# Third attention of a two-block transformer: two heads at a time, two pairs of score banks in turn, weight splits moved behind it

## The chip, the cores and the metric

One core of one Trainium2 chip. The metric is the device time of one execution in microseconds; the kernel before takes 1890.29 us (median of three runs, 1889.44 to 1892.73).

## The reference, cut to what matters

The program computes a whole two-block network on 256 tokens of width 1024. The change touches one part of it, the third of its attentions: 16 query heads of 64 share 2 key/value heads, each query sees the 128 latest keys, and a learned "sink" logit joins the softmax.

```python
def swa_mixer(x, w_qkv, sinks, w_out, pos):
    q, k, v = jnp.split(x @ w_qkv, SWA_SPLITS, axis=-1)
    q = partial_rope(q.reshape(B, S, N_HEADS_SWA, HEAD_DIM), pos)
    k = partial_rope(k.reshape(B, S, N_KV_SWA, HEAD_DIM), pos)
    ...
    o = sliding_window_gqa_sinks(q, k, v, sinks)
    return o.reshape(B, S, N_HEADS_SWA * HEAD_DIM) @ w_out

def sliding_window_gqa_sinks(q, k, v, sinks):
    s = jnp.einsum('bnqhgd,bnkhd->bnhgqk', qb, kk) * scale
    s = jnp.where(mask[None, :, None, None], s, -jnp.inf)
    mx = jnp.maximum(jnp.max(s, axis=-1), sink)
    e = jnp.exp(s - mx[..., None])
    w = e / (jnp.sum(e, axis=-1) + jnp.exp(sink - mx))[..., None]
    return jnp.einsum('bnhgqk,bnkhd->bqnhd', w, vv)
```

After it come the output projection (`c_out`), a layer norm, a mixture of 8 experts (more than half of the time) and a gated projection.

## The kernel before, in words

Each engine runs one program written out by hand, and semaphores tie them together. Products of 32-bit matrices are made in three passes: every weight chunk (128 x 2048) is loaded by SP's queue into one of four buffers `w_raw`, ScalarE rounds it to `w_hi` (`round_to`, L608), VectorE writes the rest to `w_lo` (the split, L1134), and TensorE multiplies `xt_hi` by `w_hi`, `xt_hi` by `w_lo` and `xt_lo` by `w_hi` (`rows_chunk`, L1920 to L1922). SP may load a chunk only once the chunk four places before it is split. `round_to(c)` on an engine means "do all chunks below c here". The chunks of the third attention are `c_sw` to `c_sw + 5` (block `kv`, then two query blocks `q0` and `q1`, two chunks each); `c_sw + 6` to `c_sw + 9` are those of `c_out`.

PSUM has 8 banks. Banks 0 to 3 are `acc`, two each for the even and the odd weight block; banks 4 to 7 are `scr`. The sixteen heads go in two groups g of eight. Of one head:

- TensorE, `swa_qk`: one mask matmul and two score matmuls per head, always for two heads, into banks of `scr`; then `at_qk` is raised. In a pair of these there are 2 mask matmuls and 4 score matmuls (the trace counts 8, two passes each).
- VectorE, `swa_max`: two maxima (L1429 over 128 keys, L1430 over 256 keys), a drain, and the negative maximum with the sink (L1432); then `at_negm`.
- ScalarE, `swa_prob`: two exponentials with their sums, a drain, then `at_p`. With `at_p` the score bank is free.
- TensorE, `swa_turn`: three transposes into bank `acc[q1][h % 2]`, after `at_p` of this head and the copy of the head two before; then `at_t`.
- VectorE, `turned_prob`: copies the 128 x 384 to SBUF (L1444); then `at_pt`.
- TensorE, `swa_pv`: three products with the values (L2401 to L2403), 64 wide, into `acc[q0]` for group 0 and banks 6 and 7 for group 1.

At a group's end VectorE's `attended` divides by the sums and writes `y` (L1456), TensorE transposes `y` (`turn_half`, `late_half`), ScalarE rounds the transposed half to `xt_hi` and VectorE writes `xt_lo` (`turned_at`). `rotate` is the rotary embedding of a query block on VectorE; ScalarE's `swa_block` copies a block out of PSUM before it, and `turned_queries` copies the transposed queries to `qk2` after it. `keep_warm(n)` issues n matmuls of 128x512 whose result nobody reads.

Of the kernel before, what the change touches and what calls it, by code (L numbers as in the profile page):

```python
# [23 lines left out]
P = 128  # L24
# [91 lines left out]
def build(nc, a, out, upto="end"):  # L116
# [27 lines left out]
    with ExitStack() as ctx:  # L144
# [125 lines left out]
        def swa_bank(g, h):  # L270

            return scr[:, (0, 1, 2, 3, 0, 1, 0, 1)[h] if g else h % 3, :]
# [329 lines left out]
        def _(act):  # L602
# [221 lines left out]
            def swa_prob(g, h):  # L824

                act.wait_ge(S("at_negm"), 8 * g + h + 1)
                b_, smx_ = swa_bank(g, h), smx2[:, g]
                for t, (c0, c1) in enumerate(((0, P), (P, SCW))):
                    copy((s_first, s_more)[g][:, h, c0:c1], b_[:, c0:c1], ACT.Exp, bias=smx_[:, 1, t, h:h + 1],
                         accum_out=smx_[:, 2, t, h:h + 1])  # L830
                act.drain().then_inc(S("at_p"), 1)
# [158 lines left out]
            if "qkv" in live:  # L990
# [40 lines left out]
                for t in range(NT):  # L1031
                    turned_at(8, t, 2 * t, acc[q0_b[0] % 2][t])
# [92 lines left out]
        def _(dve):  # L1125
# [299 lines left out]
            def swa_max(g, h):  # L1425

                b_, smx_ = swa_bank(g, h), smx2[:, g]
                dve.wait_ge(S("at_qk"), 8 * g + h + 1)
                dve.reduce_max(smx_[:, 0, 0, h:h + 1], b_[:, 0:P], AX_X)  # L1429
                dve.reduce_max(smx_[:, 0, 1, h:h + 1], b_[:, P:SCW], AX_X)  # L1430
                dve.drain()
                TS(smx_[:, 1, :, h:h + 1], smx_[:, 0, :, h:h + 1], sink[:, 8 * g + h:8 * g + h + 1], -1.0, ALU.max, ALU.mult)  # L1432
                dve.drain().then_inc(S("at_negm"), 1)

            def swa_sink(g):

                s8 = sink[:, 8 * g:8 * g + 8].unsqueeze(1).broadcast_to([P, NT, 8])
                TT(smx2[:, g, 3], s8, smx2[:, g, 1], ALU.add)
                dve.drain().then_inc(S("sink_ready"), 1)

            def turned_prob(g, h):

                dve.wait_ge(S("at_t"), 8 * g + h + 1)
                dve.tensor_copy(pt2[:, h % 2, :], acc[q1_b[0] % 2][h % 2][:, 0:SCW]).then_inc(S("at_pt"), 1)  # L1444
# [182 lines left out]
            if "qkv" in live:  # L1627
# [28 lines left out]
                dve.sem_inc(S("rotated"), 1)  # L1656
# [1001 lines left out]
```

## Time and profile before

| what | us |
|---|---|
| median of three runs | 1890.29 |
| the profiled execution, its own time | 1890.27 |
| its span, first to last instruction | 1888.5 |
| of it, up to the third attention's scores | 0 to 738.5 |
| scores, softmax and values of the third attention | 738.5 to 792.3 |
| output projection, norm, routing | 792.3 to 860 |
| experts and last projection | 860 to 1888.5 |

The profiled execution stands at the median of the runs. Lines in it are those of the kernel above; most ScalarE work has the helper line L608, so that its rows are told apart by their tiles (`s_first` and `s_more` are the probabilities of the two groups, `p` is `p2`, `pt` is `pt2`, `qk` is `qk2`).

### The profile page before, as it was taken

The page shows a single profiled execution, that of the slowest core. Times are in us where ns is not written, and L with a number is a line of the kernel's source. Part 1 is how long each engine was busy: PE and PEld are TensorE (multiplying, and loading weights), DVE is VectorE, ACT ScalarE, POOL GpSimd, SP SyncE. Part 2 cuts the span into 40 slices and gives each one's busy share as a digit, 9 for nine tenths or more (in the row PEclk, how much of TensorE's full clock was granted, in tenths as well). Part 3 has the DMA queues.
Part 4 walks back from the last instruction along what each step waited for, and adds up shares of the span by engine and source line. Part 5 has one row for each costly group of instructions (what it writes and reads, how often), then busy time and mean ns, then how long its engine had stood idle before and what let it go on. Part 6 is the DMA issues. An engine that isn't in the chain of part 4 may idle for free.

```text
span 1888.5 us, 24161 instructions
## 1 busy us (share of the span) xinstructions
PE 1834.6 (97%) x9844; PEld 1532.7 (81%) x9853; DVE 1394.3 (74%) x1231; ACT 1106.0 (59%) x989; POOL 61.4 (3%) x83
## 2 busy tenths in 40 slices
PE   8999999999999998899999999999999999999997
PEld 6979997897899876768788888888888888888875
DVE  4766775466645565578988888888888888888876
ACT  4545544374334344357667667676677766776772
POOL 2200000200000001000000000000000000000000
PEclk8999999999999999799999999999999999999998
DMA  7444546432555563049999999999999999999980
GB/s 250 157 153 155 178 167 212 152 129 90 174 188 180 190 206 115 24 163 387 350 367 356 344 371 349 363 363 350 369 359 341 367 352 361 364 336 375 366 307 24
DMA packets 248857, 491.02 MB, mean 260 GB/s; under 512 B 10422, under 2 KB 15610, under 8 KB 248752
## 3 DMA queue, kind: packets, MB, share of 16 engines
q1 hardware_dynamic: 244992, 477.30, 71.3%
q0 software_dynamic: 3328, 10.73, 1.7%
q8 instruction: 69, 1.13, 0.3%
q10 hardware_dynamic: 432, 1.57, 0.2%
q14 instruction: 36, 0.29, 0.0%
HBM read 487.46 MB, written 2.10 MB: 259 GB/s over the span
## 4 chain that ended last, share of the span: by engine, by line
PE 86%; DVE 8%; ACT 2%; DVEq 1%; issue 1%; DMA 0%; ACTq 0%; SPq 0%
PE psum L2518 16%; PE psum L2520 16%; PE psum L2519 16%; PE psum L1974 5%; PE psum L1977 5%; PE psum L1976 5%; PE psum L1920 5%; PE psum L1922 5%; PE psum L1921 5%; PE psum L1994 3%; DVE w_lo L1134 2%; DVE w_lo L1699 1%; ACT w_hi L608 1%; DVE xt_lo L1146 1%; DVE uv L1394 1%
## 5 line engine op out<-in xcount | busy, mean ns | idle before, releaser
L608 ACT ACTIVATE w_hi<-w_raw 128x2048 fp32r<-128x2048 f32 (+1 forms) x357 | 641.6, 1834 | 107.1 <-PE psum L1922 60.2
L1699 DVE TENSOR_TENSOR w_lo<-w_raw,w_hi 128x2048 fp32r<-128x2048 f32 (+1 forms) x238 | 511.5, 2189 | 75.3 <-ACT w_hi L608 75.2
L1134 DVE TENSOR_TENSOR w_lo<-w_raw,w_hi 128x2048 fp32r<-128x2048 f32 (+2 forms) x119 | 261.4, 2228 | 138.5 <-ACT w_hi L608 137.0
L2518 PE MATMUL psum<-w_hi,xg_hi 128*128 128x512 f32 x892 | 357.6, 401 | 1.0 <-DVE w_lo L1699 1.0
L2520 PE MATMUL psum<-w_hi,xg_lo 128*128 128x512 f32 x892 | 353.5, 396 | 0.0
L2519 PE MATMUL psum<-w_lo,xg_hi 128*128 128x512 f32 x892 | 353.5, 396 | 0.0
L1699 DVE TENSOR_TENSOR w_lo<-raw_more,w_hi 128x2048 fp32r<-128x2048 f32 (+1 forms) x118 | 254.6, 2197 | 34.8 <-ACT w_hi L608 34.5
L1974 PE MATMUL psum<-xt_hi,w_hi 128*128 128x256 f32 (+1 forms) x976 | 276.2, 283 | 1.4 <-DVE w_lo L1134 0.6
L1977 PE MATMUL psum<-xt_hi,w_lo 128*128 128x256 f32 (+1 forms) x976 | 275.7, 282 | 0.0
L1976 PE MATMUL psum<-xt_lo,w_hi 128*128 128x256 f32 (+1 forms) x976 | 274.8, 282 | 0.0
L608 ACT ACTIVATE w_hi<-raw_more 128x2048 fp32r<-128x2048 f32 (+1 forms) x118 | 212.7, 1839 | 19.3 <-PE psum L2520 18.5
L2520 PEld LDWEIGHTS psum<-w_hi,xg_lo 128*128 128x128 f32 x892 | 167.9, 188 | 40.7
L2518 PEld LDWEIGHTS psum<-w_hi,xg_hi 128*128 128x128 f32 x892 | 168.1, 188 | 40.5 <-DVE w_lo L1699 1.9
L2519 PEld LDWEIGHTS psum<-w_lo,xg_hi 128*128 128x128 f32 x892 | 168.2, 189 | 38.5
L1974 PEld LDWEIGHTS psum<-xt_hi,w_hi 128*128 128x128 f32 (+1 forms) x976 | 182.7, 187 | 4.6 <-issue 1.9
L1976 PEld LDWEIGHTS psum<-xt_lo,w_hi 128*128 128x128 f32 (+1 forms) x976 | 182.7, 187 | 0.5
L1977 PEld LDWEIGHTS psum<-xt_hi,w_lo 128*128 128x128 f32 (+1 forms) x976 | 181.6, 186 | 0.3
L2518 PE MATMUL psum<-w_hi,mh_hi 128*128 128x512 f32 x448 | 179.1, 400 | 0.2 <-DVE w_lo L1699 0.2
L2520 PE MATMUL psum<-w_hi,mh_lo 128*128 128x512 f32 x448 | 177.6, 397 | 0.0
L2519 PE MATMUL psum<-w_lo,mh_hi 128*128 128x512 f32 x448 | 177.4, 396 | 0.0
L608 ACT ACTIVATE mg<-psum 128x512 f32<-128x512 f32 x56 | 33.6, 599 | 175.4 <-PE psum L2520 175.4
L1920 PE MATMUL psum<-w_hi,xt_hi 128*128 128x512 f32 (+1 forms) x256 | 103.3, 404 | 5.0 <-DVE xt_lo L1146 3.6
(394 smaller groups left out, 2144.1 us busy)
## 6 DMA issues: line engine op xcount, KB each, us to landing
w_raw<-in_moe_w_gate_up SPq DMA_DIRECT2D x150, 1024.0 KB, 7.5
raw_more<-in_moe_w_gate_up SPq DMA_DIRECT2D x74, 1024.0 KB, 7.6
w_raw<-in_moe_w_down SPq DMA_DIRECT2D x64, 1024.0 KB, 7.4
raw_more<-in_moe_w_down SPq DMA_DIRECT2D x32, 1024.0 KB, 7.1
w_raw<-in_w_up SPq DMA_DIRECT2D x22, 1024.0 KB, 5.5
w_raw<-in_ffn_w_gate_up SPq DMA_DIRECT2D x22, 1024.0 KB, 5.5
w_raw<-in_w_in SPq DMA_DIRECT2D x12, 1024.0 KB, 5.7
w_raw<-in_ab_w_in SPq DMA_DIRECT2D x12, 1024.0 KB, 5.3
```

Source lines behind the costliest of these rows:

```text
L608: return act.activation(o, i, func, **kw)
L1134: TT(w_lo[:, k % RING, 0:n], raw(slot, n), w_hi[:, k % RING, 0:n].bitcast(F32), ALU.subtract)\
L1699: TT(w_lo[:, at, 0:n], raw(slot, n), w_hi[:, at, 0:n].bitcast(F32), ALU.subtract).then_inc(S("lo_ready"), 1)
L1920: mm(o, hi(k, t), wh, start=(k == ps[0][0]), stop=False)
L1921: mm(o, hi(k, t), wl, start=False, stop=False)
L1922: m = mm(o, lo(k, t), wh, start=False, stop=(k == kmax))
L1974: mm(o, w_hi[:, slot, cols], xt_hi[:, k, :], start=(k == 0 and c_ % 2 == 0), stop=False, skip_group_check=True)
L1976: mm(o, w_hi[:, slot, cols], xt_lo[:, k, :], start=False, stop=False, skip_group_check=True)
L1977: m = mm(o, w_lo[:, slot, cols], xt_hi[:, k, :], start=False, stop=(k == KD - 1), skip_group_check=True)
L2518: mm(o, hi[:, q, :], wh, start=(q == first), stop=False)
L2519: mm(o, hi[:, q, :], wl, start=False, stop=False)
L2520: m = mm(o, lo[:, q, :], wh, start=False, stop=(q == last))
```

## The change: heads by pairs

All three engines now step by pairs p = 0 to 7 (two heads each).

- The scores of pair p go to banks 4 and 5, then 6 and 7, in turn; pair 7 goes to banks 2 and 3 (`acc[q0]`), after `at_y`, that is once the first group's result has been taken from there. Pair 1's scores have a bank pair of their own, so they wait for no probability; pair p's scores wait for `at_p` of pair p - 2.
- `swa_max` takes both heads in one instruction per key range (128x2x128 and 128x2x256), and one instruction with a negated sink makes the two negative maxima.
- `swa_prob` does both heads' four exponentials before its one drain and signal.
- `swa_turn` makes six transposes into banks 0 and 1 (`acc[q1]`) and waits for the copy of the pair before; `turned_prob` copies both heads (128x768) at once; `swa_pv` makes six products. The transposes thus have one pair of banks instead of two single banks in turn.
- ScalarE copies block q1 right after pair 0's probabilities (before: after five heads), VectorE rotates it after two pairs' maxima and before any copy (before: after eight heads' maxima and one copy), TensorE turns its queries right behind pair 0's transposes. 4 warming matmuls stand there instead of 8.
- VectorE splits chunk `c_sw + 6` after all maxima and seven of the eight copies (before: after three heads' maxima), and `c_sw + 7` after the last copy; ScalarE rounds `c_sw + 7` after the probabilities instead of between the groups.
- The first transposed half of `y` goes to banks 4 and 5 instead of `acc[q0]`.

The core of the diff, cut:

```diff
+        def swa_pair(p):
+            b_ = (4, 6, 4, 6, 4, 6, 4, 2)[p]
+            return psum[:, b_:b_ + 2, 0:SCW]
...
 (ScalarE)
-                for h in range(5):
-                    swa_prob(0, h)
+                swa_prob(0)
                 swa_block(q1_b)
-                for h in range(5, 8):
-                    swa_prob(0, h)
-                turned_queries(4, 7)
+                swa_prob(1)
+                turned_queries(4, 6)
                 turned_queries(6, 7)
+                for p in range(2, 4):
+                    swa_prob(p)
                 swa_sink(0)
-                round_to(c_sw + 8)
-                for h in range(8):
-                    swa_prob(1, h)
+                for p in range(4, 8):
+                    swa_prob(p)
                 swa_sink(1)
...
                 round_to(c_sw + 9)
 (VectorE)
+            def swa_max(p):
+                g, hs = p // 4, slice(2 * (p % 4), 2 * (p % 4) + 2)
+                dve.wait_ge(S("at_qk"), 2 * p + 2)
+                dve.reduce_max(smx2[:, g, 0, 0, hs], swa_pair(p)[:, :, 0:P], AX_X)
+                dve.reduce_max(smx2[:, g, 0, 1, hs], swa_pair(p)[:, :, P:SCW], AX_X)
+                dve.drain()
+                STT(smx2[:, g, 1, :, hs], smx2[:, g, 0, :, hs], -1.0, sink[...], ALU.mult, ALU.min)
+                dve.drain().then_inc(S("at_negm"), 1)
+            def turned_prob(p):
+                dve.wait_ge(S("at_t"), p + 1)
+                dve.tensor_copy(pt2[:], turned_pair[:, :, 0:SCW]).then_inc(S("at_pt"), 1)
...
+                swa_max(0)
+                swa_max(1)
                 wait_evacuated(dve, q1_b[0])
                 rotate(NB, 8)
+                for p in range(4):
+                    turned_prob(p)
+                    swa_max(p + 2)
+                    if p == 1:
+                        swa_sink(0)
+                turned_prob(4)
                 attended(0)
+                swa_max(6)
+                turned_prob(5)
+                swa_max(7)
+                turned_prob(6)
                 swa_sink(1)
+                round_to(c_sw + 7)
+                for t in range(NT):
+                    turned_at(8, t, 2 * t, scr[:, t, :])
+                turned_prob(7)
                 round_to(c_sw + 8)
                 attended(1)
 (TensorE)
+                    if 5 <= k < 7:
+                        swa_qk(k - 5)
                 rows_chunk(q1_b, 1, xh, xl, between=scores_between)
+                swa_qk(2)
                 wait_evacuated(pe, q1_b[0])
+                swa_turn(0)
+                keep_warm(4, 3)
+                pe.wait_ge(S("at_p"), 2)
+                turn_queries(4, 6)
                 turn_queries(6, 7)
+                swa_pv(0)
+                swa_turn(1)
+                for p in range(1, 6):
+                    swa_qk(p + 2)
+                    swa_pv(p)
+                    swa_turn(p + 1)
+                for t in range(NT):
+                    turn_half(y, 0, t, scr[:, t, :])
+                swa_pv(6)
+                swa_turn(7)
+                swa_pv(7)
```

TensorE, one round of the steady part. Before, two heads of the second group, with the semaphores on which each row waits; a row without a name for one follows the row before it:

```order
L2378 MATMUL psum<-mask_126,ident_127 128x384 [waits at_p]
L2378 MATMUL psum<-mask_126,ident_127 128x384
L2381 MATMUL psum<-qk_123 128x128 x2
L2381 MATMUL psum<-qk_123 128x256 x2
L1994 MATMUL psum<-ident,s_first 128x128 [waits at_pt,at_p]
L1994 MATMUL psum<-ident,s_first 128x128 x2
L2401 MATMUL psum<-p_122,pt_124 128x64 [waits at_pt]
L2402 MATMUL psum<-p_122,pt_124 128x64
L2403 MATMUL psum<-p_122,pt_124 128x64
L1994 MATMUL psum<-ident,s_first 128x128 [waits at_pt,at_p]
L1994 MATMUL psum<-ident,s_first 128x128 x2
L2401 MATMUL psum<-p_122,pt_124 128x64 [waits at_pt]
```

and in the changed kernel, one pair:

```order
L2384 MATMUL psum<-mask_126,ident_127 128x384 [waits at_p]
L2384 MATMUL psum<-mask_126,ident_127 128x384
L2387 MATMUL psum<-qk_123 128x128 x2
L2387 MATMUL psum<-qk_123 128x256 x2
L2413 MATMUL psum<-p_122,pt_124 128x64 [waits at_pt]
L2414 MATMUL psum<-p_122,pt_124 128x64
L2415 MATMUL psum<-p_122,pt_124 128x64
L2413 MATMUL psum<-p_122,pt_124 128x64
L2414 MATMUL psum<-p_122,pt_124 128x64
L2415 MATMUL psum<-p_122,pt_124 128x64
L1996 MATMUL psum<-ident,s_first 128x128 [waits at_pt,at_p]
L1996 MATMUL psum<-ident,s_first 128x128 x5
```

The same matmuls for two heads now stand in three runs, scores, products, transposes, with one wait each. Between a transpose and the product that needs its copy stand the scores of a later pair, where before there was one head's transposes at most places.

VectorE at the end of the stage. Before, from the last copy but four:

```order
L1438 TENSOR_TENSOR smx_131<-sink,smx_131 128x16
L1134 TENSOR_TENSOR w_lo<-w_raw,w_hi 128x2048 [waits hi_ready]
L1444 COPY pt_124<-psum 128x384 [waits at_t] x3
L1153 TENSOR_TENSOR xt_lo<-psum,xt_hi 128x4x128 [waits xt_hi_ready] x2
L1444 COPY pt_124<-psum 128x384 [waits at_t]
L1450 TENSOR_TENSOR smx_131<-smx_131 128x16 [waits at_sum]
```

and in the changed kernel, from the last copy but one:

```order
L1449 COPY pt_124<-psum 128x768 [waits at_t]
L1443 TENSOR_TENSOR smx_131<-smx_131,sink 128x16
L1138 TENSOR_TENSOR w_lo<-w_raw,w_hi 128x2048 [waits hi_ready]
L1157 TENSOR_TENSOR xt_lo<-psum,xt_hi 128x4x128 [waits xt_hi_ready] x2
L1449 COPY pt_124<-psum 128x768 [waits at_t]
L1138 TENSOR_TENSOR w_lo<-w_raw,w_hi 128x2048 [waits hi_ready]
L1455 TENSOR_TENSOR smx_131<-smx_131 128x16 [waits at_sum]
```

One split (`c_sw + 6`) and both parts of `xt_lo` now stand between the last two copies, and a second split (`c_sw + 7`) between the last copy and the second `attended`.

## Rows read from the trace of the kernel before

**Rows 1.** The page: busy us of each engine (share) xinstructions.

```profile
PE 1834.6 (97%) x9844; PEld 1532.7 (81%) x9853; DVE 1394.3 (74%) x1231; ACT 1106.0 (59%) x989; POOL 61.4 (3%) x83
```

**Rows 2.** TensorE's waits from 738.5 to 792.5: total us, times, longest.

```profile
PE psum L2401 <- DVE pt L1444: 6.5, 7, 2.2
PE psum L2378 <- ACTq L831: 3.8, 3, 2.9
```

**Rows 3.** Windows: busy us (instructions) by engine, granted clock, DMA share, GB/s.

```profile
746.70:749.64 2.94, 0.00 (x1) 0.01 (x1) 2.46 (x9) 1.83 (x8) 0.00 (x0) 1.00 0.52 163
749.64:753.30 3.66, 3.63 (x16) 2.18 (x16) 1.27 (x5) 2.37 (x9) 0.00 (x0) 0.54 0.41 158
...
770.50:773.90 3.40, 1.29 (x10) 0.98 (x9) 2.92 (x9) 0.92 (x4) 0.00 (x0) 0.99 0.00 0
773.90:794.30 20.40, 18.12 (x80) 16.06 (x81) 11.40 (x24) 5.95 (x16) 0.00 (x0) 0.50 0.16 52
```

**Rows 4.** TensorE in time: start, us, line, operation; at the full clock.

```profile
738.52 0.50 PE L2378 MATMUL psum<-mask,ident 128*128 128x384 bf16 x2
...
739.81 0.50 PE L1920 MATMUL psum<-w_hi,xt_hi 128*128 128x512 f32 x1
...
741.97 0.50 PE L2378 MATMUL psum<-mask,ident 128*128 128x384 bf16 x2 [0.49 <-ACTq L831]
...
755.47 1.67 PE L1999 MATMUL psum<-ones_tri 128*128 128x512 bf16 x7
756.98 0.60 PE L1994 MATMUL psum<-ident,p 128*128 128x128 f32 x4
757.42 0.49 PE L1994 MATMUL psum<-ident,s_first 128*128 128x128 f32 x3
757.75 0.33 PE L2401 MATMUL psum<-p,pt 128*128 128x64 f32 x2
...
758.36 0.61 PE L1994 MATMUL psum<-ident,p 128*128 128x128 f32 x4
...
759.75 0.49 PE L2378 MATMUL psum<-mask,ident 128*128 128x384 bf16 x2
...
761.02 0.55 PE L1994 MATMUL psum<-ident,s_first 128*128 128x128 f32 x3
```

**Rows 5.** TensorE in time, the stage's end; at the half clock.

```profile
791.08 0.63 PE L2401 MATMUL psum<-p,pt 128*128 128x64 f32 x2
...
792.32 0.77 PE L1920 MATMUL psum<-w_hi,xt_hi 128*128 128x512 f32 x1
```

**Rows 6.** VectorE in time: maxima, a split, the first `attended`.

```profile
739.98 0.29 DVE L1429 TENSOR_REDUCE smx<-psum 128x1 f32<-128x128 f32 x1 [5.29 <-PE psum L2381]
740.19 0.41 DVE L1430 TENSOR_REDUCE smx<-psum 128x1 f32<-128x256 f32 x1
...
741.03 0.29 DVE L1429 TENSOR_REDUCE smx<-psum 128x1 f32<-128x128 f32 x1
...
744.40 2.29 DVE L1134 TENSOR_TENSOR w_lo<-w_raw,w_hi 128x2048 fp32r<-128x2048 f32 x1
...
771.69 0.17 DVE L1450 TENSOR_TENSOR smx<-smx 128x16 f32<-128x16 f32 x1
...
773.67 0.29 DVE L1429 TENSOR_REDUCE smx<-psum 128x1 f32<-128x128 f32 x1
```

**Rows 7.** VectorE groups of 380 to 560 us: shapes, busy, mean ns.

```profile
L1550 DVE COPY pt<-psum 128x384 f32<-128x384 f32 x8 | 4.4, 554 | 4.3 <-PE psum L1994 4.3
...
L1476 DVE TENSOR_TENSOR stick<-psum,mask_sb 128x768 f32<-128x768 f32 x4 | 3.8, 956 | 0.4 <-PE psum L2213 0.2
```

**Rows 8.** ScalarE in time, one head's exponentials and the next.

```profile
740.98 0.37 ACT L608 ACTIVATE s_first<-psum,smx 128x128 f32<-128x128 f32 x1 [1.32 <-DVEq L1433]
...
742.02 0.37 ACT L608 ACTIVATE s_first<-psum,smx 128x128 f32<-128x128 f32 x1
```

**Rows 9.** TensorE's waits after 860 us.

```profile
PE psum L2518 <- DVE w_lo L1699: 0.2, 1, 0.2
```

More of the change, by code:

```diff
@@ L2370, in turn_queries, with swa_qk @@
                     i.then_inc(S("swa_t"), 1)
-                def swa_qk(g, h):
-                    if g or h >= 2:
-                        pe.wait_ge(S("at_p"), (8, 8, 10, 14)[h // 2] if g else h - 1)
-                    pair = (h, h + 1)
-                    for u in pair:
-                        mm(swa_bank(g, u)[:, 0:SCW], ident_16[:], mask_16[:], start=True, stop=True)
+                def swa_qk(p):
+                    if p >= 2:
+                        pe.wait_ge(S("at_p"), p - 1)
+                    if p == 3:
+                        pe.wait_ge(S("qk2_ready"), 5)
+                    if p == SWA_PAIRS - 1:
+                        pe.wait_ge(S("at_y"), 1)
+                    g, to = p // 4, swa_pair(p)
+                    for u in range(2):
+                        mm(to[:, u, :], ident_16[:], mask_16[:], start=True, stop=True)
@@ L2379, in swa_qk @@
                     for t, (c0, c1) in enumerate(((0, P), (P, SCW))):
-                        for u in pair:
-                            i = mm(swa_bank(g, u)[:, c0:c1], qk2[lane(u), 4 * g + u // 2, t * P:(t + 1) * P],
-                                   qk2[lane(u), 8 + g, 0:c1 - c0], start=False, stop=True, skip_group_check=True)
+                        for u in range(2):
+                            i = mm(to[:, u, c0:c1], qk2[lane(u), p, t * P:(t + 1) * P], qk2[lane(u), 8 + g, 0:c1 - c0],
+                                   start=False, stop=True, skip_group_check=True)
@@ L2399, in swa_pv @@
+                def swa_pv(p):
+                    pe.wait_ge(S("at_pt"), p + 1)
+                    g = p // 4
+                    if p == 4:
+                        pe.wait_ge(S("at_p"), 6)
                     v = lambda t: p2[:, t, SWA_V + g * DH:SWA_V + (g + 1) * DH]
                     to = [scr[:, 2 + t, :] for t in range(NT)] if g else acc[q0_b[0] % 2]
-                    mm(to[0][:, o], pt2[:, h % 2, 0:P], v(0), start=True, stop=True)
-                    mm(to[1][:, o], pt2[:, h % 2, P:SEQ], v(0), start=True, stop=False)
@@ L2403, in swa_pv @@
-                    m = mm(to[1][:, o], pt2[:, h % 2, SEQ:SCW], v(1), start=False, stop=True)
-                    if h == 7:
+                    for u in range(2):
+                        o = slice((2 * (p % 4) + u) * DH, (2 * (p % 4) + u + 1) * DH)
+                        mm(to[0][:, o], pt2[:, u, 0:P], v(0), start=True, stop=True)
+                        mm(to[1][:, o], pt2[:, u, P:SEQ], v(0), start=True, stop=False)
+                        m = mm(to[1][:, o], pt2[:, u, SEQ:SCW], v(1), start=False, stop=True)
@@ L2405, in swa_pv @@
+                    if p % 4 == 3:
                         m.then_inc(S("at_o"), 1)
```

109 lines of the change are left out of this document (23 added, 86 removed).

## The prediction

> **What bounds the kernel now.** The page first: TensorE is busy 97% of the span [rows 1], so the end moves only by what TensorE's program gains or loses, and only where it stands still or runs slowly. The list of waits for the stage of the third attention's scores, softmax and values shows where it stands still: ten stops with 10.3 us in total, seven for VectorE's copy of the transposed probabilities (6.5 us) and three for ScalarE's probabilities, whose banks the next scores need (3.8 us) [rows 2]. The windows show where it runs slowly: after the stop of 746.70 to 749.64 the granted clock is half until about 753.3, and after the window 770.5 to 773.9, in which TensorE was busy 1.29 of 3.40 us, it is half, 1.2 GHz, up to 794.3 [rows 3]. The reader is to see in rows 3 that in this last stretch TensorE is busy 18.12 of 20.40 us and the clock still does not rise; it does only when the dense weight products of `c_out` have run for 2 us, from 792.32 [rows 3, 5]. So a stop costs twice here, once itself and once by the slow clock behind it.
>
> The stage reaches from TensorE's first scores, 738.52 [rows 4], to the first product of `c_out`, 792.32 [rows 5]: 53.8 us. In pieces, at the full clock, by differences of starts in rows 4: the scores of two heads 1.27 (759.75 to 761.02), three transposes 0.33 (757.42 to 757.75), a head's products 0.61 (757.75 to 758.36), four transposes of queries or of `y` 0.44 (756.98 to 757.42), a warming matmul 0.22 to 0.24 (seven in 1.67), six weight products between scores 1.5 (739.81 to the stop that ends at 741.97 after 0.49). The work is then 8 x 1.27 + 16 x 0.33 + 16 x 0.61 + 4 x 0.44 + 8 x 0.22 + 2 x 1.5 = 31.8. The half clock adds 1.7 in 749.64 to 753.3 (3.63 busy for one pair's scores and six transposes, 1.93) and half of what is busy from 773.9 to 792.32, 18.12 less the 2.0 behind 792.32, so 8.1: together 9.8 [rows 3, 5]. With 10.3 of stops that is 51.9; the missing 1.9 I put down to the tail and the restart at ten stops, 0.2 each.
>
> **The change, part by part.** *Work on TensorE:* the same matmuls, four warming ones fewer: -0.9.
>
> *A steady round.* TensorE needs 1.27 + 2 x 0.61 + 2 x 0.33 = 3.15 for a pair. VectorE: a head's maxima come every 1.05 us (739.98 to 741.03) [rows 6]; from 128 to 256 elements a maximum grows from 0.29 to 0.41, so a pair's two grow by 0.12 and 0.27, together 1.45. A copy of 128x384 takes 0.554, and the nearest row to one of 128x768 is an addition from PSUM of that size, 0.956 [rows 7]. Bounds for the paired copy: not under 0.9 (the slope of rows 6 over 384 more elements, 0.36, on 0.554), not over 1.11 (two copies); I take 0.96, since element count sets both rows. VectorE's round is 2.4 us. ScalarE needs 1.04 for a head (740.98 to 742.02) [rows 8], so a pair at most 2.08, and with one drain fewer some 1.85. Both are below 3.15: TensorE sets the round, if no chain does. Chain one: six transposes end, 0.1 to VectorE, copy 0.96, 0.05 back, 1.1 to 1.2, against the 1.27 of scores that stand between: it fits by 0.1. With the copy at 1.11 it just misses and costs up to 0.1 a round. Chain two: scores, 0.1, maxima to ScalarE 1.00 + 0.39 (739.98 to 740.98, plus the growth) [rows 6, 8], probabilities 1.8, so 3.3, against 4.4 us of other work before that pair's transposes: it fits by 1.1.
>
> The Trainium skill (Perfetto Trace Analysis, Optimizing Scalar/DVE Operations) counts about 125 ns of overhead for each VectorE instruction on PSUM and says that larger ones help if the engine is saturated. By it 8 copies and 16 maxima fewer give an estimate of 3 us, and nothing if VectorE isn't the bound; VectorE is busy 1.27 of 3.66 us in the first slow stretch [rows 3], so the rule would price the edit near nothing. Rows 6 and 7 put the saving at about 0.15 per merged instruction, but what counts is whom a pair releases, and when.
>
> *The stops, followed in time.* Pair 1's scores wait for nothing now (0.5 gone), pair 2's wait for `at_p` of pair 0, ready at 743.2, before TensorE comes at 744.2. ScalarE copies block q1 when it ends (744.4), 1.0 us, VectorE rotates it for 1.85 (as now), so the queries can be turned at 747.4; TensorE has six transposes and four warming matmuls until 747.0 and waits 0.4. That replaces the stop of 2.94 [rows 3] and the 1.3 behind it. The split of `c_sw + 6`, 2.29 [rows 6], that stood between heads 2 and 3 of VectorE's maxima, at 744.40, is out of that chain. Then rounds of 3.15 without a stop until pair 5. There the first `attended`, 1.98 on VectorE (771.69 to 773.67) [rows 6], stands before pair 6's maxima and pair 5's copy: TensorE waits 0.9 for the copy, then 0.3 for the next one. By this count, restarts aside, its transposes of pair 7 are issued at 770.2.
>
> *The last stop is new.* Behind pair 6's copy VectorE splits `c_sw + 6` (2.29), makes two `xt_lo` (0.6 each at their pace) and only then copies pair 7, so 2.3 + 1.2 + 1.0 = 4.5 from 768.4: 772.9. TensorE waits 2.7. Behind it are only pair 7's products and `c_out`, whose operands are ready by then. The split of `c_sw + 7` ends at 775 and `attended` delivers at 776.4, before `c_out` has got to the transposes that want it, 2.8 us of products after 774.1 at the full clock: hidden, by 0.5. SP's load of the first expert chunk waits for the split of `c_sw + 6` and so starts 24 us later (770.7 for 746.7); it is needed only behind `c_out`, whose own weight products take over 22 us, and the routing, so hidden too.
>
> All stops: 0.4 + 0.9 + 0.3 + 2.7 + 0.3 of small ones = 4.6, with seven restarts of 0.1.
>
> *The clock.* With no early stop over 1 us I expect it full up to the last stop. That one, 2.7, is like the 2.94 after which it fell. Then pair 7's products take 2.4 instead of 1.2 (791.08 to 792.32 is one head's, 1.24) [rows 5], and `c_out` begins slow, as it does now. So half clock: 9.8 before, 1.2 after.
>
> **The sum.** Stops 4.6 for 10.3, -5.7; restarts 0.7 for 1.9, -1.2; half clock 1.2 for 9.8, -8.6; warming -0.9: -16.4. Behind the stage nothing absorbs it: after 860 us TensorE waits once, 0.2 us, for a weight split [rows 9]. The profiled execution took 1890.27, as the median: 1890.3 - 16.4 = 1873.9.
>
> **The rivals.** *The clock stays up to the end* (the last stop falls otherwise than the 2.94 did, as the 1.3 of 753.3 left it up): 1.2 less, and `c_out`'s first twelve products, about 1.0 slow now, at full pace: 1871.7. I give it 0.32, and the forecast 0.44.
>
> *VectorE or ScalarE is the bound of the round:* copies at 1.11 or more and maxima 0.2 dearer: five rounds and the last chain lose 0.3 to 0.5 each, so 1876.5. Against it: rows 7. 0.10.
>
> *The clock falls midway,* at the stop of 0.9 for pair 5's copy: 5.9 us of work behind it take twice as long, some 2.5 of which hides the last stop: +3.4, 1877.5; a fall one or two rounds earlier 3 us more each, 1880 to 1884. For it: transposes and narrow products did not raise the clock in 20 us [rows 3]. 0.09.
>
> *Slower:* the same mechanism from the start. The clock falls while TensorE waits for ScalarE's copy and the rotation (745.5 to 747.4) and stays half up to `c_out`: 24.1 us of work from 745.4 on double, 4.2 of stops are swallowed: +19.9 against a gain of 17.6 at full clock, 1892.6, and past 0.2% with a rotation 1.5 us later than counted. It decides once 17.6 us of work run slow. Against it: 0.4 of stop for the 2.94 that it took before. 0.03, of it 0.02 beyond 0.2%.
>
> *The gain does not reach the end,* since the late splits hold `c_out` or the experts' loads start late: then 3 to 17 us are lost, 1877 to 1890. Against it: the margins above. 0.02.
>
> **How the numbers follow.** The two likeliest cases span 1870.5 to 1875 with the copy's bounds; 8 in 10 need some of the third and the fourth: 1870 to 1879.5. Runs before spread by 3.3 us, and 0.2%, 3.8 us, is about what a measurement can tell from no change. Faster by more: 0.95; within: 0.03; slower: 0.02.
>
> **What would show it.** In the profile after: no stop over 1 us on TensorE before pair 7's products; rounds of 3.1 to 3.3 us; the pair's copy at 0.96, its maxima 0.41 and 0.68; a stop of 2 to 3.5 us before the last six products with VectorE in split, `xt_lo`, copy; the clock full up to there; `c_out`'s first product near 776. Wrong it would be with half clock inside the rounds, stops for `at_p`, or waits on w_lo in `c_out`.

## The result and the profile after

The changed kernel takes 1876.64 us, median of four runs (1872.35 to 1877.07); the kernel before, run beside it, 1889.87 (1887.90 to 1892.73). The ratio is 0.992 with a 95% interval of 0.9904 to 0.9936. In a second set it took 1875.78 against 1891.67, ratio 0.9924 (0.991 to 0.9937). It is faster, by 13 to 16 us; 1873.9 was forecast, with 1870.0 to 1879.5 as its range.

The kernel before has no single time either: beside the experiments its medians were 1888.12, 1891.48 and 1891.67. In the last of these sets six executions took 1886.76 to 1888.23, with a mean granted clock of 0.988 to 0.991, and eleven 1891.40 to 1893.36, with 0.985 to 0.987. Of the changed kernel's ten executions one took 1872.35, the others 1875.30 to 1877.07.

The profiled execution took 1876.83, its span is 1874.7. On its page TensorE is as full as in [rows 1], with 7.5 us less of busy time, and VectorE and ScalarE have lost little:

```profile
PE 1827.1 (97%) x9840; PEld 1527.8 (81%) x9849; DVE 1388.8 (74%) x1200; ACT 1105.0 (59%) x989; POOL 61.6 (3%) x83
```

TensorE's waits from 738 to 790 (total us, times, longest), the list that answers to [rows 2]:

```profile
PE psum L2413 <- DVE pt L1449: 3.3, 3, 2.3
PE psum L1996 <- DVEq L1648: 0.2, 1, 0.2
```

Ten stops with 10.3 us have become four with 3.45 (0.15, 0.78, 0.18 and 2.34), none of them for ScalarE's probabilities. The windows, in the columns of [rows 3], show the clock full (1.00) while the stops are short, and half behind the last one:

```profile
770.00:775.00 5.00, 2.48 (x21) 2.07 (x19) 4.88 (x7) 4.45 (x5) 0.00 (x0) 1.00 0.17 31
775.00:776.00 1.00, 1.00 (x7) 1.00 (x7) 1.00 (x1) 0.45 (x1) 0.00 (x0) 0.62 1.03 401
776.00:782.00 6.00, 6.00 (x18) 5.01 (x19) 2.78 (x5) 0.00 (x0) 0.92 (x1) 0.50 0.79 265
782.00:783.00 1.00, 1.00 (x8) 0.79 (x7) 0.00 (x0) 0.06 (x1) 0.00 (x0) 0.97 0.02 2
```

TensorE in time: rounds, the last stops, the stage's end, and the half transposes of `y` that follow `c_out`'s first twelve products.

```profile
751.68 0.49 PE L2384 MATMUL psum<-mask,ident 128*128 128x384 bf16 x2
752.10 0.93 PE L2387 MATMUL psum<-qk 64*128 64x128 f32 x8
752.95 0.43 PE L2413 MATMUL psum<-p,pt 128*128 128x64 f32 x2
...
754.34 0.82 PE L1996 MATMUL psum<-ident,s_first 128*128 128x128 f32 x6
755.00 0.49 PE L2384 MATMUL psum<-mask,ident 128*128 128x384 bf16 x2
...
767.10 0.43 PE L2413 MATMUL psum<-p,pt 128*128 128x64 f32 x2 [0.78 <-DVE pt L1449]
...
774.91 0.43 PE L2413 MATMUL psum<-p,pt 128*128 128x64 f32 x2 [2.34 <-DVE pt L1449]
...
777.23 0.77 PE L1922 MATMUL psum<-w_hi,xt_hi 128*128 128x512 f32 x1
...
782.31 0.60 PE L1996 MATMUL psum<-ident,y 128*128 128x128 f32 x4
```

The reader is to see three things. A round (one pair's scores, another's products, a third's transposes) is 3.32 us (751.68 to 755.00), without a stop; the first stop inside a round is the 0.78 at 767.10, behind the first `attended`. The stop before pair 7's products is 2.34, and those products then take 2.32 (774.91 to 777.23). And `c_out`'s twelve products need 5.08 up to 782.31. In the trace of before the same point is this row, 3.78 behind the first product of [rows 5]:

```profile
796.10 0.60 PE L1994 MATMUL psum<-ident,y 128*128 128x128 f32 x4
```

From this point on the time is the same: 1092.4 us remain to the end of the span in both traces (1888.5 - 796.10, 1874.7 - 782.31).

VectorE in time says why the last stop is there: the pair's copy stands behind a split and two `xt_lo`.

```profile
766.96 0.41 DVE L1433 TENSOR_REDUCE smx<-psum 128x2 f32<-128x256 f32 x1
767.29 0.68 DVE L1434 TENSOR_REDUCE smx<-psum 128x2 f32<-128x512 f32 x1
...
770.50 2.29 DVE L1138 TENSOR_TENSOR w_lo<-w_raw,w_hi 128x2048 fp32r<-128x2048 f32 x1
772.71 1.28 DVE L1157 TENSOR_TENSOR xt_lo<-psum,xt_hi 128x512 fp32r<-128x512 f32 x2
773.91 0.95 DVE L1449 COPY pt<-psum 128x768 f32<-128x768 f32 x1
774.78 2.28 DVE L1138 TENSOR_TENSOR w_lo<-w_raw,w_hi 128x2048 fp32r<-128x2048 f32 x1
```

The span is 13.8 us shorter, in three pieces: the stage from first scores to `c_out`'s first product takes 37.37 instead of 53.80 (739.86 to 777.23), -16.4; the twelve products take 5.08 instead of 3.78, +1.3; and the stage begins at 739.86 instead of 738.52, +1.3, though nothing ahead of it was changed.

### The profile page after: what moved, and what is told of

Read it like the earlier page. It is cut to its first block, busy times and chain, and to the rows that moved or that the text cites. A ratio compares the mean times of both kernels' runs of the same rounds, so it can differ in the third digit from the quotient of the medians.

```text
span 1874.7 us, 24092 instructions
## 1 busy us (share of the span) xinstructions
PE 1827.1 (97%) x9840; PEld 1527.8 (81%) x9849; DVE 1388.8 (74%) x1200; ACT 1105.0 (59%) x989; POOL 61.6 (3%) x83
## 4 chain that ended last, share of the span: by engine, by line
PE 87%; DVE 7%; ACT 2%; issue 1%; DVEq 1%; DMA 0%; ACTq 0%; SPq 0%
PE psum L2511 17%; PE psum L2513 17%; PE psum L2512 17%; PE psum L1976 5%; PE psum L1979 5%; PE psum L1978 5%; PE psum L1922 5%; PE psum L1923 5%; PE psum L1924 5%; PE psum L1996 3%; DVE w_lo L1138 2%; ACT w_hi L611 1%; DVE w_lo L1701 1%; DVE uv L1398 1%; PE psum L2485 1%
## 5 line engine op out<-in xcount | busy, mean ns | idle before, releaser
L611 ACT ACTIVATE w_hi<-raw_more 128x2048 fp32r<-128x2048 f32 (+1 forms) x118 | 212.7, 1838 | 19.0 <-PE psum L2513 18.5
```

The source lines that it names most:

```text
L611: return act.activation(o, i, func, **kw)
```

## The experiments

All times are medians. "Stage" is from the first scores to `c_out`'s first product, "twelve" the twelve products behind it, both in the run's one profiled execution. "Before" is the median of the kernel before in the same set; the ratio compares the runs of one set and is not the quotient of the two medians. The changed kernel itself stood in the first and in the last set only (a2_again), so differences of less than some 2 us between other rows and it are read from stage and twelve.

| run | us | before | ratio to before, 95% | stage | twelve |
|---|---|---|---|---|---|
| before (profile) | | | | 53.80 | 3.78 |
| changed | 1876.64 | 1889.87 | 0.992 [0.9904, 0.9936] | 37.37 | 5.08 |
| e1_fill | 1872.44 | 1888.12 | 0.9907 [0.9887, 0.9927] | 36.43 | 2.89 |
| e2_split_first | 1872.68 | 1888.12 | 0.991 [0.9891, 0.9929] | 35.13 | 2.89 |
| e3_both_splits | 1876.91 | 1888.12 | 0.9933 [0.9914, 0.9952] | 39.85 | 3.81 |
| e4_one_pair | 1885.88 | 1888.12 | 0.9977 [0.9965, 0.999] | 48.47 | 4.42 |
| b1_split_alone | 1888.5 | 1891.48 | 0.9992 [0.9981, 1.0004] | 50.64 | 2.89 |
| e5_single_ops | 1876.76 | 1891.48 | 0.9921 [0.99, 0.9942] | 37.88 | 5.05 |
| e6_block_late | 1875.47 | 1891.48 | 0.9921 [0.9903, 0.994] | 38.02 | 4.43 |
| e7_no_stop | 1874.24 | 1891.48 | 0.9908 [0.9891, 0.9925] | 35.17 | 4.51 |
| a2_again | 1875.78 | 1891.67 | 0.9924 [0.991, 0.9937] | 37.39 | 5.07 |
| e2_again | 1872.6 | 1891.67 | 0.9902 [0.9886, 0.9918] | 35.15 | 2.88 |
| b2_fill | 1887.66 | 1891.67 | 0.9983 [0.9974, 0.9992] | 49.16 | 4.39 |
| e8_own_buffer | 1871.43 | 1891.67 | 0.9896 [0.988, 0.9912] | 33.89 | 2.89 |

**e1_fill: ten warming matmuls in the last stop.**

```diff
                 swa_turn(7)
+                keep_warm(10, 3)
                 swa_pv(7)
```

> The changed kernel with ten warming matmuls (128x512, bank 3) issued behind pair 7's transposes, in the last stop of 2.34 us. Nothing waits for them. Theory (a stop costs itself and then the slow clock behind it): the time until pair 7's products stays as it is, but the granted clock stays full there and in c_out; pair 7's products take 1.3 instead of 2.3 us and the first twelve products of c_out 2.8 instead of 4.8, so 3.0 us less than the changed kernel in a run like its profile (1877 to 1874). Rival (the clock falls for the long run of transposes and narrow products, not for the stop): the half clock comes all the same, 0 us. Second rival (the fillers only push the products back): up to 0.2 us more.

The filler takes 2.32 us, a stop of 0.18 remains, pair 7's products take 1.36 and the clock is 1.00 from 770 to 790:

```profile
771.01 2.32 PE L2001 MATMUL psum<-ones_tri 128*128 128x512 bf16 x10
773.51 0.43 PE L2413 MATMUL psum<-p,pt 128*128 128x64 f32 x2 [0.18 <-DVE pt L1449]
...
774.87 0.48 PE L1922 MATMUL psum<-w_hi,xt_hi 128*128 128x512 f32 x1
```

The filler does no work and takes as long as the stop, and 0.94 are gained in the stage and 2.19 in the twelve products, 3.1 together. So the half clock was a consequence of the standstill, and cost 3.1 us in the changed kernel. All four executions stand between 1870.77 and 1873.06, where nine of the changed kernel's ten took 1875.30 or more.

**e2_split_first, and again as e2_again: the split of `c_sw + 6` ahead of pair 0's maxima.**

```diff
                 dve.drain()
+                round_to(c_sw + 7)
                 swa_max(0)
```

> The changed kernel with the split of chunk c_sw+6 ahead of pair 0's maxima, where VectorE idles 5.2 us, instead of behind pair 6's copy. Theory: pair 0's maxima are some 0.7 us later and nobody waits for it; the last stop loses the 2.3 us of the split down to the bare chain of transposes, copy, products, so 2.34 becomes 1.0 to 1.3, and at that length the clock stays full: 1.2 + 3.0 = 4 us less than the changed kernel, about 1872.5. Rival: the stop gets shorter but the clock falls all the same, only 1.2 us less. Rival: the early split delays pair 0's probabilities so that a stop appears at pair 2's scores or the rotation, and 0.5 to 1 us of it is given back.

> The changed kernel with the split of c_sw + 6 ahead of pair 0's maxima, again, to have it beside the changed kernel in one set: 4 us less than the changed kernel by my theory (1.3 of stop, 1.0 in pair 7's products, 1.9 in the first twelve products of c_out), the stop of 1.05 again with the clock up behind it. If the clock falls behind it this time, 1 to 2 us less.

The last stop is 1.05 in both profiles, the clock stays at 1.00 to 790, and VectorE's 2.29 us there delay nobody. In the last set, beside the changed kernel, 1872.60 against 1875.78: 3.2 less where 4 were expected. Stage and twelve are 2.2 shorter each, 4.4 in all, but this profile reached the stage 1.6 later than that of a2_again (740.32 against 738.70). The waits of the first:

```profile
PE psum L2414 <- DVE pt L1449: 2.0, 3, 1.0
PE psum L1997 <- DVEq L1648: 0.2, 1, 0.2
```

**e3_both_splits: the split of `c_sw + 7` ahead of pair 7's copy too,** so that the last stop doubles.

```diff
-                turned_prob(7)
                 round_to(c_sw + 8)
+                turned_prob(7)
```

> The changed kernel with the split of c_sw+7 ahead of pair 7's copy as well: the suspected delay of the last stop doubled. Theory: the last stop grows by 2.2 us to 4.6; behind it the clock is half as already now, so 2.2 us more than the changed kernel, up to 1 more if the half clock lasts longer. Rival (the stop is not on the path, as TensorE would wait for c_out's operands anyway): 0.

The wait and the window:

```profile
PE psum L2413 <- DVE pt L1449: 5.5, 3, 4.5
```

```profile
774.00:780.00 6.00, 4.11 (x16) 3.82 (x17) 3.30 (x6) 0.23 (x1) 0.00 (x0) 0.50 0.86 302
```

2.2 us more of stop make the stage 2.5 longer but the twelve products 1.3 shorter, since the clock fell near 773.7, inside the stop, and part of its slow time passed while TensorE stood. Together that is 1.2 more. The median is 0.3 above the changed kernel's in the first set and 1.1 above that in the last, in neither case the +2.2 that I expected: a longer stop doesn't price the slow clock behind it anew.

**e4_one_pair: the scores of pair p wait for the probabilities of pair p - 1,** as if there were one pair of score banks.

```diff
                     if p >= 2:
-                        pe.wait_ge(S("at_p"), p - 1)
+                        pe.wait_ge(S("at_p"), p)
```

> The changed kernel, but the scores of pair p wait for the probabilities of pair p-1 instead of pair p-2, as if there were one pair of score banks. Theory (two pairs in turn are what keeps TensorE from stopping): the chain scores, maxima, probabilities, 3.3 us, has then to fit into one pair's products and transposes, 1.9 us, so five rounds stop 1.3 to 1.6 us each, 7 to 8 us in all, and more with a slower clock, up to 15: 1884 to 1892, most of the gain gone. Rival (pairing of instructions is the gain, banks are not): under 2 us.

Six stops for ScalarE come back, the largest, 2.81, at the place of the 2.94 of [rows 3], and behind it the clock is at 0.55 in 748 to 755:

```profile
PE psum L2384 <- ACTq L836: 8.2, 6, 2.8
PE psum L2413 <- DVE pt L1449: 2.3, 1, 2.3
```

```profile
748.00:755.00 7.00, 7.00 (x32) 4.62 (x32) 2.14 (x5) 0.55 (x2) 0.00 (x0) 0.55 0.00 1
```

11.1 of the 16.4 us of the stage go, 7.1 of them as stops (10.5 for 3.45), as expected, and the rest by the clock, which is half again from 778.2 to 781.5. With everything else of the change in place, the second bank pair so carries two thirds of the gain, the half clock that it keeps away included. How much that clock weighs varies: two of the ten executions took 1879.88 and 1880.00, with a mean granted clock of 0.992 and 0.993, the other eight 1885.43 to 1887.17, with 0.989 or 0.990.

**b1_split_alone: the kernel before, with only the split of `c_sw + 6` moved ahead of the maxima.**

```diff
+                round_to(c_sw + 7)
-                for h in range(3):
-                    swa_max(0, h)
-                round_to(c_sw + 7)
-                for h in range(3, 8):
+                for h in range(8):
                     swa_max(0, h)
```

> The kernel before, with one thing of the change alone: VectorE's split of chunk c_sw + 6 stands ahead of the first head's maxima instead of between heads 2 and 3. My theory (the chain per head and three banks make the early stop, the split only lengthens it): head 3's maxima come 2.2 us earlier, but head 4's scores end at about 746.7 as now, so its maxima come at 746.7, its probabilities end near 748.6 and the scores of heads 6 and 7 start at 748.7 instead of 749.64; the stop of 2.94 becomes 2.0, and the time falls by 1 us, by at most 3 if the clock stays up behind the shorter stop, up to some 10 us if it stays up to the end. Rival (most of the change's gain is the split's place, not the pairs): the stop vanishes, the clock never falls early, and the time comes near that of the changed kernel, 12 to 14 us less.

TensorE, at the scores of heads 6 and 7:

```profile
749.38 0.52 PE L2376 MATMUL psum<-mask,ident 128*128 128x384 bf16 x2 [2.01 <-ACTq L831]
```

The stop is 2.01, as counted, and the interval of the ratio holds 1, so the rival, 12 to 14 us less, is wrong. The split made the stop longer, it did not make it. That the chain per head with its three banks did is what is left; for the banks e4_one_pair shows it, in the order by pairs. Another stop grew, since the early split delays the first maxima, and the stops of the stage sum to 10.8, for 10.3:

```profile
742.64 0.50 PE L2376 MATMUL psum<-mask,ident 128*128 128x384 bf16 x2 [1.17 <-ACTq L831]
```

Yet the stage of this profile is 3.2 shorter. Its last stretch of half clock, behind stops of the same lengths as before (1.31 and 2.23), ended at 783.8 and not at 794.3:

```profile
774.00:783.60 9.60, 7.73 (x34) 6.06 (x35) 5.08 (x12) 3.55 (x14) 0.00 (x0) 0.50 0.00 0
```

Whether the split or the single execution did that isn't shown. Five of the ten executions took 1886.28 to 1887.47 and five 1889.52 to 1891.22, two groups like those of the kernel before.

**e5_single_ops: order and signals by pairs, VectorE's instructions per head.**

```diff
-                dve.reduce_max(smx2[:, g, 0, 0, hs], swa_pair(p)[:, :, 0:P], AX_X)
-                dve.reduce_max(smx2[:, g, 0, 1, hs], swa_pair(p)[:, :, P:SCW], AX_X)
+                for u in range(2):
+                    h = 2 * (p % 4) + u
+                    dve.reduce_max(smx2[:, g, 0, 0, h:h + 1], swa_pair(p)[:, u, 0:P], AX_X)
+                    dve.reduce_max(smx2[:, g, 0, 1, h:h + 1], swa_pair(p)[:, u, P:SCW], AX_X)
...
-                dve.tensor_copy(pt2[:], turned_pair[:, :, 0:SCW]).then_inc(S("at_pt"), 1)
+                for u in range(2):
+                    i = dve.tensor_copy(pt2[:, u], turned_pair[:, u, 0:SCW])
+                i.then_inc(S("at_pt"), 1)
```

> The changed kernel with its order and its signals by pairs, but VectorE's instructions per head again: four maxima of a pair instead of two, two copies of 128x384 (0.55 each at their own pace) instead of one of 128x768. A pair's maxima then take about 1.36 instead of 1.10 and its copy 1.11 instead of 0.96. My theory (TensorE sets the round, the order is what gains): the copy still ends within 0.1 us of when TensorE has done the scores in between; 0 to 0.1 per round, 0.3 at the first attended and 0.15 to 0.4 at the last stop: 0.5 to 1 us slower than the changed kernel. Rival (fewer and larger VectorE instructions are what gains): 3 us slower or more, with VectorE's busy time in the stage up by that and stops of TensorE for the copy in each round.

The pair's two copies take 1.02 for 0.96, the stage is 0.5 longer, the waits for the copy are 3.6 for 3.3, at the same three places, and no round has got a new one. So of the 16.4 us the merging of VectorE's instructions brings 0.5; the rest is banks, order and the signals by pairs. (ScalarE's exponentials stayed by pairs in this run.)

```profile
770.45 1.02 DVE L1452 COPY pt<-psum 128x384 f32<-128x384 f32 x2 [1.01 <-PE psum L2000]
```

**e6_block_late: ScalarE's copy of block q1 behind pair 1's exponentials.**

```diff
-                swa_block(q1_b)
                 swa_prob(1)
+                swa_block(q1_b)
```

> The changed kernel with ScalarE's copy of block q1 behind pair 1's exponentials, not ahead of them. Pair 1's maxima are there at 745.35, so the copy starts near 747.1 instead of 745.64 and TensorE stops some 1.3 us before pair 0's transposes and 0.3 to 0.4 at the queries, 1.5 us in all. My theory (what matters is that a stop early in the stage stays short; the clock stayed up behind stops of 1.05 us): plus 1.5 us if the clock stays up; rival, in which a stop of 1.3 to 1.5 is already enough to lose the clock at the start: half clock from the first rounds on, 3 to 17 us more than the changed kernel.

```profile
PE psum L2413 <- DVE pt L1449: 3.3, 3, 2.3
PE psum L1996 <- ACT p L611: 1.6, 1, 1.6
PE psum L1996 <- DVEq L1648: 0.2, 1, 0.2
```

```profile
745.00:750.00 5.00, 3.27 (x26) 2.08 (x22) 2.63 (x12) 2.28 (x9) 0.00 (x0) 1.00 0.01 2
...
777.00:780.00 3.00, 3.00 (x9) 2.31 (x8) 2.21 (x5) 0.00 (x0) 0.09 (x1) 0.53 0.60 179
```

The new stop is there, 1.6, and the clock stays at 1.00 behind it; the rival that it would fall is wrong here. But the time didn't rise by 1.5 (the median is 1.2 below the changed kernel's in the first set, 0.3 below that in the last): behind the last stop, again 2.34, the clock fell only in 777 to 778 and pair 7's products still ran in 1.36, which gave 1.0 back, and the twelve gave 0.65. The same stop, in the same place of the program, was followed by 6.8 us of half clock in the two profiles of the changed kernel and by 3.4 in this one and in that of e4_one_pair.

**e7_no_stop: on top of the early split, the half transposes of `y` between pair 7's transposes and its products, and pair 7's copy ahead of the `xt_lo`.**

```diff
+                round_to(c_sw + 7)
                 swa_max(0)
...
+                turned_prob(7)
                 for t in range(NT):
                     turned_at(8, t, 2 * t, scr[:, t, :])
-                turned_prob(7)
...
-                for t in range(NT):
-                    turn_half(y, 0, t, scr[:, t, :])
                 swa_pv(6)
                 swa_turn(7)
+                for t in range(NT):
+                    turn_half(y, 0, t, scr[:, t, :])
                 swa_pv(7)
```

> The changed kernel with the split of c_sw + 6 ahead of pair 0's maxima, and at the end the products of pair 6 and the transposes of pair 7 ahead of the four half transposes of y on TensorE, and pair 7's copy ahead of the two xt_lo on VectorE. The early split alone left a stop of 1.05 us. Now the copy starts when pair 7's transposes end and lies beside 0.9 us of half transposes: the stop falls to 0.2 to 0.4, so 0.7 us less than with the early split alone, about 5 us less than the changed kernel. Rival: the xt_lo, now 1 us later, hold the first product of c_out back by as much, and nothing is gained over the early split alone.

TensorE's rows with a wait behind 770:

```profile
770.66 0.43 PE L2414 MATMUL psum<-p,pt 128*128 128x64 f32 x2 [1.05 <-DVE pt L1449]
773.92 0.43 PE L2414 MATMUL psum<-p,pt 128*128 128x64 f32 x2 [0.18 <-DVE pt L1449]
779.83 0.66 PE L1997 MATMUL psum<-ident,y 128*128 128x128 f32 x4 [1.43 <-DVEq L1465]
```

A miss that neither theory had. The stop of 1.05 is gone from pair 7 and has come at pair 6, whose copy the half transposes had covered before: there are 0.9 us of cover for two copies. And VectorE's split now began at 776.26, 36.1 us after the first scores, where it began 33.8 after them with the early split alone, so the second `attended` behind it was late for `c_out`: 1.43. The `xt_lo` held the first product back by nothing (it follows pair 7's products, 775.32), so the rival's cause is wrong too. The stage is no shorter than with the early split alone (35.17 for 35.13), and the twelve are 1.6 longer, most of it the new stop.

**a2_again: the changed kernel, unchanged.**

> The changed kernel once more, unchanged, beside the others of this set. In its first profile the stage began 1.3 us later than before, and its time ahead differs from that of before by the granted clock alone: 0.91 in 130 to 150 us, behind the same stop of about 4 us that left it at 1.00 in other profiles. My theory (whether a given stop drops the clock is not the same in each execution of one program): the times fall into groups 3 to 5 us apart, the stage starts near 738.4 or 740 according to the clock at 130 to 150, and the length of the half clock behind the last stop is again between 3 and 7 us. Rival: the same program has the same clock in each execution; then start and slow stretch are those of the first profile within 0.2 us.

The window 130 to 150, first of the changed kernel's first profile, then of this one, and TensorE at 140:

```profile
130.00:150.00 20.00, 16.59 (x98) 11.79 (x98) 13.46 (x19) 9.29 (x15) 1.07 (x2) 0.91 0.39 125
```

```profile
130.00:150.00 20.00, 15.96 (x106) 11.48 (x106) 12.84 (x18) 9.15 (x15) 1.07 (x2) 1.00 0.43 144
```

```profile
140.53 1.97 PE L1996 MATMUL psum<-ident,y 128*128 128x128 f32 x8 [2.65 <-DVEq L1196]
```

```profile
140.00 1.09 PE L1996 MATMUL psum<-ident,y 128*128 128x128 f32 x8 [2.65 <-DVEq L1196]
```

Behind the same stop of 2.65 the same eight transposes take 1.97 in one execution and 1.09 in the other, and the stage starts at 739.86 or 738.70. Of these 1.2 us half, 0.5, is there ahead of the transposes already (140.53 for 140.00), where the clock of the kernel's first microseconds rose at 20.9 in one execution and at 19.7 in the other. So the 1.3 us that the first profile had lost ahead of the stage are no effect of the change. Stage and twelve are as before (37.39, 5.07), and the last half clock lasts 6.8 again. The times did not fall into groups in this set (1875.30 to 1876.69); there my expectation missed, though the first set had one at 1872.35.

**b2_fill: the kernel before, with filler in three stops.**

```diff
+                def fill(n):
+                    for _ in range(n):
+                        mm(psum[:, 7, 256:512], busy[:, 0:P], busy[:, 256:512], start=True, stop=True)
+
+                fill(24)
                 swa_qk(0, 6)
...
+                fill(10)
                 swa_pv(1, 0)
                 swa_turn(1, 2)
+                fill(18)
                 swa_pv(1, 1)
```

> The kernel before with narrow filler products (128x256 into a free half bank, 0.11 us each) in three of its stops: 24 ahead of the scores of heads 6 and 7 (2.94 us), 10 ahead of head 8's products (1.31), 18 ahead of head 9's (2.23). The order by heads and all other instructions stay. My theory (about half the change's gain is clock, and a fast clock needs only that the stops be short or filled): the clock stays at full through the stage, the 9.8 us of half clock go, and 1 to 3 us come back as longer stops for the copies, which the slow TensorE had hidden behind 776: 1881 to 1884. Rival (the slow clock comes of the narrow work itself, not of the stops): the clock falls all the same, and the time is that of before or up to 1 us more.

```profile
742.00:785.00 43.00, 35.96 (x276) 26.64 (x277) 28.34 (x79) 21.92 (x74) 0.00 (x0) 1.00 0.08 27
785.00:792.00 7.00, 7.00 (x32) 6.42 (x31) 3.94 (x8) 0.00 (x0) 0.69 (x1) 0.54 0.43 144
```

```profile
PE psum L2401 <- DVE pt L1444: 5.7, 7, 1.9
PE psum L2378 <- ACTq L831: 1.1, 3, 0.5
```

The mechanism is right: full clock to 785, where the narrow work of before had half of it for 20 us. The size is wrong: 1881 to 1884 was expected, 1887.66 came. The stage is 4.6 shorter, not 9.8. The stops are now 6.8 and the fillers 6.2, 13.0 for 10.3, so 2.7 came back as waiting, as expected. But the clock fell after all behind late stops of 1.21 and 1.43, at 785.6, which costs 1.8 in the stage and 0.6 in the twelve products, and this profile began the stage 1.4 later than that of before. Of the 8.0 us that the clock gave back in the stage 2.7 returned as waiting and 0.7 aren't accounted for. So in the order by heads about a third of them was cover for VectorE's and ScalarE's chains: there a fast clock turns in part into waiting.

**e8_own_buffer: the early split, pair 7's copy in a buffer of its own, its transposes ahead of pair 6's products.**

```diff
-                dve.tensor_copy(pt2[:], turned_pair[:, :, 0:SCW]).then_inc(S("at_pt"), 1)
+                dve.tensor_copy(s_first[:, 0:2, :] if p == 7 else pt2[:], turned_pair[:, :, 0:SCW]).then_inc(S("at_pt"), 1)
...
+                turned_prob(7)
                 for t in range(NT):
                     turned_at(8, t, 2 * t, scr[:, t, :])
-                turned_prob(7)
-                round_to(c_sw + 8)
                 attended(1)
+                round_to(c_sw + 8)
...
-                swa_pv(6)
                 swa_turn(7)
+                swa_pv(6)
                 swa_pv(7)
```

> The changed kernel with the early split, and with pair 7's transposed probabilities copied into a buffer of their own (heads 0 and 1 of s_first, read long ago). So TensorE transposes pair 7 ahead of pair 6's products, whose 1.34 us cover VectorE's copy of 0.96, which stands ahead of the xt_lo; the second attended stands ahead of the split of c_sw + 7, so that c_out's half transposes find y. Expected: the stop of 1.05 gone, c_out's first product 34.1 us after the first scores instead of 35.1 with the early split alone, no stop over 0.3 us in c_out: 1.0 us less than with the early split alone, near 1871. Rival: the split of c_sw + 7 now ends at 777 and holds c_out's second chunk or its half transposes, and the gain is lost there.

```profile
PE psum L2415 <- DVE pt L1449: 0.8, 1, 0.8
PE psum L1997 <- DVE pt L1449: 0.3, 1, 0.3
PE psum L1997 <- DVEq L1648: 0.2, 1, 0.2
```

The stage is 33.89, 1.26 less than with the early split alone, no wait follows in `c_out`, and the median is 1871.43 against 1872.60, the lowest of this study and 4.4 below the changed kernel in the same set. The rival is wrong.

## Why the prediction held, and what it mis-sized

**The mechanism** held at each step that it named: two bank pairs take away the waits for `at_p` (e4_one_pair brings them back, with the early half clock), the rounds run without a stop up to the first `attended` and wait 0.78 and 0.18 behind it, where 0.9 and 0.3 were counted, the pair's copy is 0.96 and its maxima 0.41 and 0.68, the one large stop stands before pair 7's products behind split and `xt_lo`, and the clock falls there. That the split's old place was not the cause is shown by b1_split_alone; that merging instructions is worth little, by e5_single_ops. The estimate of 3 us from the Trainium skill (Perfetto Trace Analysis, Optimizing Scalar/DVE Operations) would have needed VectorE as the bound; the stage lost 0.5 without the merging.

**The stage** was to take 53.8 - 16.4 = 37.4 and takes 37.37, but two terms were off and cancel. Stops: 4.6 counted, 3.45 measured; the queries wait 0.15 and not 0.4, the last stop is 2.34 and not 2.7. Against that a round takes 3.32, not 3.15: a pair's six products take 1.39 (752.95 to 754.34), where I had doubled the 0.61 of one head; over seven pairs that is the 1.2 which the restarts were to hold only in part. The 0.61 is that of products right behind transposes, whose first takes 0.16 to the next (757.75 to 757.91); behind scores the first takes 0.27 (752.95 to 753.22), and the second head's three take 0.67. Half clock in the stage: 1.0 measured (2.32 against 1.36 for pair 7's products in e1_fill), 1.2 counted. That the sum came out within 0.1 is thus luck in part.

**The step that failed** is the one on the clock: "`c_out` begins slow, as it does now". It does, but for 5.08 us in the twelve products instead of 3.78, and 2.89 at full clock. In the trace before the clock had been slow for 18.5 us when `c_out` began and rose 2.0 us into it; now it had fallen only 2.0 us before (near 775.2), and it stayed down for 6.8. The slow clock behind the last stop so cost 3.1 us in all, where the sum had 1.2 in the stage and nothing new in `c_out`. That is +1.3 of the miss of 2.7 in the first set's median.

**The other part** of the miss in the profiled execution, 1.3 ahead of the stage, belongs to the single execution, as a2_again shows. How often an execution draws the one or the other isn't settled by these runs, so the remaining 0.6 to 1.4 between the medians and the forecast corrected by 1.3 stays open. The forecast's start, 1890.3, is a draw of the same kind: against the kernel before of the same set the gain is 13.2 and 15.9, where 16.4 was forecast.

**A caveat on the sum.** "Half clock -8.6" was right as an entry of account, but not as a cause that works alone: b2_fill took 8.0 of the 9.8 us out of the stage of the kernel before and gained 4.6. What makes a short stage possible at full clock is the change to pairs (35.1 in e2_split_first, against 49.2 in b2_fill). And the 8.1 us of half clock at the old stage's end were read from one execution; in b1_split_alone, whose tail is the same program, that stretch was 10.2 us long instead of 20.5.

**Not tested alone** are the second bank pair in the order by heads, the earlier copy and rotation of block q1 (e6_block_late moves the copy by one step only), and ScalarE's one drain per pair. The third of the stage's gain that neither e4_one_pair nor e5_single_ops accounts for isn't divided among them.

**A row too few.** The list of TensorE's waits after 860 us holds more than its row in [rows 9]: 0.3 us for VectorE, and before the last projection, at 1842 and 1855, one of 2.0 and one of 6.3. In the changed kernel's trace they are 1.9 and 8.0: between them the clock was half for a while in the first trace (0.57 from 1842 to 1846) and full in the second, and the longer wait took that up. Of the change they absorbed nothing, since the 1092.4 us to the end are the same in both traces.

## What to carry to other kernels

Follow the semaphore that frees a bank: a second bank pair, which lets the scores run two rounds ahead of the softmax, brought two thirds of this gain (the half clock that it keeps away included), and fewer, larger VectorE instructions 0.5 us. When a change ends a stall, put the deferred work where its engine idles (here VectorE's 5 us before the first maxima), not in front of the last item of a chain, and check each cover (the work that hides another engine's) for whom it covered before. Price a stop like the 2.34 here together with the half clock behind it, 3 us more; but don't count all slow time as gain: b2_fill got 4.6 of 9.8 us. And take more than one profile before explaining 1 or 2 us: compare the granted clock of parts that nobody changed.

## What the runs showed of the hardware

One program doesn't have one clock. Behind the stop of 2.65 us at 140 us, the same in every kernel here, the granted clock of 130 to 150 us was 1.00 in seven profiles of the fourteen and 0.91 in the other seven. The two kinds differ earlier too: in the seven with 1.00 the half clock of the kernel's first microseconds had ended by 19.8 us and that stop by 140.00; in the seven with 0.91 it ended at 20.4 us or later, and the stop at 140.31 or later. So the outcome went with the moment at which the stop came; why, these runs don't show.

Behind the last stop of 2.34 us (2.41 in e5_single_ops) the clock was half (1.2 GHz) for 6.8 us in three profiles, beginning 0.3 us behind the stop's end, and for 3.4 us in two, e4_one_pair and e6_block_late, beginning 1.8 behind it. Stops of 1.05 (e2_split_first), 1.6 (e6_block_late) and 1.93 (b2_fill, at 755) left it full; one of 2.01 (b1_split_alone, at 749) was followed by half clock, and in b2_fill so were 1.21 and 1.43, 4.5 us apart. A stop of 4.54 was no dearer afterwards than one of 2.34: the twelve products took 3.81 against 5.08.
